# DeltaNet core: identity folded into the fp16 matrices, half-width inversion levels, and two heads side by side

## What is computed

```python
L = where(strict, einsum('bhncd,bhnsd->bhncs', k * beta, k) * decay, 0)
sol = triangular_solve(eye + L, concatenate([v * beta, k * beta * exp(g)]))
u, w = split(sol)
qk = where(tril, einsum('bhncd,bhnsd->bhncs', q, k) * decay, 0)
def step(S, xs):
    v_new = u_i - einsum('bhcd,bhde->bhce', w_i, S)
    o = einsum(qd_i, S) + einsum(qk_i, v_new)
    S = S * gl_i + einsum('bhcd,bhce->bhde', kd_i, v_new)
```

## Time and profile before

| | |
|---|---|
| median of 3 runs | 5612.43 us (5612.35 to 5614.2) |
| span of the profiled execution | 5611.9 us |
| PE, PEld, DVE, ACT, POOL busy | 4687.5, 3852.9, 3332.0, 2146.1, 2161.1 us |
| the phase of the delta core | about 1840 to 3932 us of the span |
| mean granted TensorE clock | 0.925 of full speed |

### The profile page before, as it was taken

One profiled execution on the slowest core, in us unless ns is written; L12 is line 12 of the kernel. 1 busy time (PEld: TensorE's weight loads), 2 busy tenths in 40 slices (PEclk: granted clock), 3 DMA queues, 4 the chain that ended last, 5 costly groups with the idle time before them and its releaser, 6 DMA issues. The chain is left out here.

```text
span 5611.9 us, 92238 instructions
## 1 busy us (share of the span) xinstructions
PE 4687.5 (84%) x32058; PEld 3852.9 (69%) x32058; DVE 3332.0 (59%) x3990; ACT 2146.1 (38%) x3371; POOL 2161.1 (39%) x1544
## 2 busy tenths in 40 slices
PE   7479889988998688888888888888599759975649
PEld 1467777777777577777777777777488548864547
DVE  1414543455334688888888888888455443339854
ACT  0212222232223455555555555555211231137732
POOL 0311111111121666777666767675211132213222
PEclk8569999999999899999999999999799879987879
DMA  4102212212222333333333333332544212221134
GB/s 203 48 25 70 58 49 69 81 46 64 65 69 62 92 95 95 92 92 92 95 95 94 92 93 93 95 93 77 186 174 177 102 54 68 66 94 69 67 103 135
DMA packets 587420, 503.28 MB, mean 90 GB/s; under 512 B 115200, under 2 KB 556544, under 8 KB 573184
## 3 DMA queue, kind: packets, MB, share of 16 engines
q1 hardware_dynamic: 587296, 501.82, 29.7%
HBM read 351.00 MB, written 150.67 MB: 89 GB/s over the span
## 5 line engine op out<-in xcount | busy, mean ns | idle before, releaser
L448 PE MATMUL pj_bank<-h_hi,pj_whi 128*128 128x512 f32 (+1 forms) x1920 | 716.5, 373 | 19.7 <-POOL pj_wlo L434 19.7
L448 PE MATMUL pj_bank<-h_lo,pj_whi 128*128 128x512 f32 (+1 forms) x1920 | 707.8, 369 | 0.0
L448 PE MATMUL pj_bank<-h_hi,pj_wlo 128*128 128x512 f32 (+1 forms) x1920 | 707.3, 368 | 0.0
L1215 DVE TENSOR_TENSOR dc_Y<-dc_psY,dc_levels 128x512 f16<-128x512 f32 x864 | 554.3, 683 | 117.3 <-PE dc_psY L996 113.8
L1219 DVE TENSOR_TENSOR dc_X<-dc_psX,dc_X 128x512 f16<-128x512 f32 x864 | 575.8, 690 | 79.6 <-PE dc_psX L1010 48.4
L431 POOL TENSOR_TENSOR pj_whi<-pj_w,ones 128x1024 fp32r<-128x1024 f32 x48 | 126.8, 2642 | 1192.4 <-DMA pj_w<-in_gdn_w_in 959.0
L1129 ACT ACTIVATE dc_R<-dc_psR 128x512 f16<-128x512 f32 x864 | 492.5, 596 | 123.2 <-PE dc_psR L1006 112.8
L622 ACT ACTIVATE pj_raw<-pj_bank 128x512 f32<-128x512 f32 (+1 forms) x240 | 129.0, 555 | 1005.6 <-PE pj_bank L448 634.9
L448 PEld LDWEIGHTS pj_bank<-h_hi,pj_whi 128*128 128x128 f32 x1920 | 362.9, 189 | 82.9 <-POOL pj_wlo L434 20.1
L912 POOL TENSOR_TENSOR dc_bm<-dc_dec,dc_bm 128x512 f32<-128x512 f32 x144 | 183.3, 1273 | 588.1 <-ACT dc_dec L1106 587.9
L448 PEld LDWEIGHTS pj_bank<-h_lo,pj_whi 128*128 128x128 f32 x1920 | 363.0, 189 | 62.6 <-issue 3.8
(11 more groups left out here) (239 smaller groups left out, 11155.3 us busy)
## 6 DMA issues: line engine op xcount, KB each, us to landing
dc_tm<-scratch_tm SPq DMA_DIRECT2D x288, 192.0 KB, 2.4
dc_fm<-scratch_fm SPq DMA_DIRECT2D x288, 128.0 KB, 2.6
dc_cgr<-scratch_cgrow SPq DMA_DIRECT2D x288, 128.0 KB, 2.9
scratch_o<-dc_ob SPq DMA_DIRECT2D x288, 128.0 KB, 1.9
scratch_tm<-pj_tm SPq DMA_DIRECT2D x24, 1152.0 KB, 6.3
mod_w<-in_mod_w SPq DMA_DIRECT2D x16, 1536.0 KB, 30.2
pj_w<-in_gdn_w_in SPq DMA_DIRECT2D x48, 512.0 KB, 7.4
scratch_fm<-pj_row SPq DMA_DIRECT2D x16, 1152.0 KB, 6.0
```

The costliest lines, as they stand in the source:

```text
L448: i = pe.matmul(self.bank[blk][:, 0:n], l[b][:, k, :], r[:, k, at:at + n], start=(m == 0), stop=(m == 3 * KT - 1))
L1215: dve.tensor_tensor(Y[p][:], bY[p][:], lev_r(l + 1), ALU.mult).then_inc(eY[p], 1)
```

## The change

Only `phase_delta_core` changes. Its parts are:

1. **Half columns.** A level of block size s = 2^l changes only half of the columns of R and X, the other half only of Y. Y, R and X products of levels 2 to 6 are now made for 64 of the 128 columns of each of the four problems, side by side in 256 columns of a bank (`quart`), and the copies out of PSUM take those 256 elements and write them to their places in the 512 (`all_cols`, runs of s elements). Products of Y and the first transposes (`first`) are half wide from the start; R and X of level 1 are full.
2. **Identity inside.** A = Lhi + I in fp16, Y keeps the identity in the columns that are not written (one Y tile for each level, filled once at the start), so that X Y alone is the new R and the identity products of the levels (L1004) and of the error (L1018) go. X is no longer an addition on DVE but a copy: level 1 on DVE, levels 2 to 6 on ACT.
3. **Level 0** is made by masking A instead of multiplying and adding: still two fp16 operations on DVE, both with two SBUF inputs.
4. **Making.** `gram` is read once from PSUM by DVE under a mask of both triangles (`masked`, new, 128x512); ACT's copy L1115 and POOL's L907 and L913 go. `scores` now has two SBUF inputs.
5. **Two heads side by side.** p = 0 and 1 are two different q/k heads at the same chunk, so that each has its own state, and only the banks Z and V tie them. The order of the pieces of the recurrence in a level changes accordingly.
6. **SyncE** issues the same 28 transfers in an iteration, written out for all 72 without a loop, at other distances ahead (recurrence 1, `fm` 3, rows 4).

```diff
+        quart = lambda t: t[:].rearrange("p d h t -> p (d h t)")[:, 0:2 * P]
+        def cols(t, c, l, own):
+            o = (c // 2 == 0) == own
+            return comb(t, c).rearrange("p (b o s) -> p b o s", o=2, s=1 << l)[:, :, 1 if o else 0, :]
+        def all_cols(t, l, of_r):
+            s = 1 << l
+            at, step = (s, 2 * P - s) if of_r else (0, 2 * P + s)
+            a = t[:]
+            return bass.AP(tensor=a.tensor, offset=a.offset + at, ap=[[4 * P, P], [step, 2], [2 * s, P // s], [1, s]])
+        def split4(v, l):
+            return v.rearrange("p (d b s) -> p d b s", d=2, s=1 << l)
+        pick, x0m = sb("pick", [P, LV] + H4[1:], F16), sb("x0m", [P, 2, P], F16)
+        R0 = two("R0", H4, F16)
+        Y = [two(f"Y{l}_", C4, F16) for l in range(1, NLEV)]
...
                 def level_y(j, q, l, p):
+                    for c in range(4):
+                        m = pe.matmul(quart(bY[p])[:, c * 64:(c + 1) * 64], comb(A[q][p], c),
+                                      half(R0[p], c) if l == 1 else cols(R[p], c, l, True), start=True, stop=True)
...
                 def level_rx(j, l, p):
-                    pe.matmul(flat(bR[p]), id16[:, 0:P], flat((R0 if l == 0 else R)[p]), start=True, stop=False)
+                    for c in range(4):
+                        if l == 1:
+                            m = pe.matmul(comb(bR[p], c), comb(X0[p], c), comb(y, c), start=True, stop=True)
+                        else:
+                            m = pe.matmul(quart(bR[p])[:, c * 64:(c + 1) * 64], comb(X[p], c), cols(y, c, l, True), start=True, stop=True)
...
                 def newton_e(j, q, p):
-                    pe.matmul(flat(bY[p]), id16[:, 0:P], flat(R[p]), start=True, stop=False)
...
                 @sweep
                 def run(i, q, ahead, make, inv, rec):
+                    for l in range(1, NLEV):
+                        if inv:
+                            for p in range(2):
+                                level_y(j, r, l, p)
+                        if rec and l <= 2:
+                            state_by_k(i, q, l - 1)
+                        if rec and l in (3, 4):
+                            solved(i, l - 3)
+                        if rec and l == 6:
+                            update(i, q, 1)
+                        if inv:
+                            for p in range(2):
+                                level_rx(j, l, p)
+                        if make and l <= 2:
+                            gram(i + 2, q, l - 1)
+                        if rec and l == 4:
+                            update(i, q, 0)
+                        if rec and l >= 5:
+                            outputs(i, q, 0, l - 5)
...
                 def level_x(j, l, p):
+                    act.activation(all_cols(X[p], l, False), split4(quart(bX[p]), l), ACT.Copy).then_inc(eX[p], 1)
...
                 def masked(j, q, p):
+                    dve.tensor_tensor(gm[q][p][:], bV[:], sides[:], ALU.mult).then_inc(s_gm[p], 1)
                 def level(j, l, p):
-                    dve.tensor_tensor(Y[p][:], bY[p][:], lev_r(l + 1), ALU.mult).then_inc(eY[p], 1)
+                    dve.tensor_tensor(all_cols(Y[l - 1][p], l, True), split4(quart(bY[p]), l),
+                                      split4(pick[:, l - 1].rearrange("p c t -> p (c t)"), l), ALU.mult).then_inc(eY[p], 1)
```

More of the change, by code:

```diff
@@ L766, in phase_delta_core @@
[L766 to L773, removed]
@@ L805, in run @@
                     for q in range(2):
                         body(m * 2 + q, q, True, True, True, True)
-                for i in range(NPAIR - 4, NPAIR):
+                for i in range(NI - 4, NI):
                     at(i)
             return run
[L811 to L817, removed]
@@ new lines, in store, with step @@
+                def store(m, n, p):
+                    row = m * 2 + p
+                    wait(sp, s_ob[p], m * NCH + n + 1)
+                    for dr in range(2):
+                        dst = dram["o"][dr, chunk(dr, n)].rearrange("p (q h) t -> p q h t", h=2)[:, bass.ds(row, 1)]
+                        sp.dma_start(dst.rearrange("p o h t -> p (o h) t"), ob[p][:, dr]).then_inc(s_out[p], 16)
+                def step(m, n, last):
+                    for load, ahead in ((load_rec, 1), (load_fm, 3), (load_row, 4)):
+                        if not (last and n + ahead >= NCH):
+                            for p in range(2):
+                                load(*place(m, n, ahead), p)
+                    for p in range(2):
+                        store(m, n, p)
@@ L967, in _ @@
+                    for p in range(2):
+                        if ahead:
+                            differences(i + 3, 1 - q, p)
+                        if make:
+                            low(i + 2, q, p)
+                        if inv:
+                            beta_v(i + 1, 1 - q, p)
                 run(pool)
@@ new lines, in run @@
+                            if l == 1:
+                                for p in range(2):
+                                    level_x(j, p)
+                        if rec and l == 1:
+                            right_side(i, q, 0)
+                        if rec and l in (3, 4):
+                            faded_v(i, q, l - 3)
+                        if make and l in (1, 2):
+                            masked(i + 2, q, l - 1)
+                        if rec and l == 2:
+                            right_side(i, q, 1)
@@ L1267, in run @@
+                        if make and l in (3, 4):
+                            scores(i + 2, q, l - 3)
+                        if make and l in (5, 6):
+                            first(i + 2, q, l - 5)
+                        if rec and l == 5:
+                            state(i, q, 0)
+                    if rec:
+                        state(i, q, 1)
                     if inv:
```

614 lines of the change are left out of this document (299 added, 315 removed).

## The result

The changed kernel takes 5250.9 us (median of 4 runs, 5248.2 to 5253.1) against 5613.3 us before (4 runs): ratio 0.935, 95% interval 0.934 to 0.937. I had forecast 5395 us, with a range of 5280 to 5520. The sign was right; the size was wrong, and so was the range. The change saved 362 us where I had 217.

What follows compares the result with a forecast made beforehand. It took a PE, DVE, PE, ACT chain on two nearly full engines as the bound; iterations of 28.56 us becoming 25.5 save 3.06 us times 71, 217 us, so 5611.9 becomes 5395 us, range 5280 to 5520.

Steps and rivals of the forecast that it cites:

- the term for PE: PE work per delta-core iteration: 24.1 to 21.0 us, identity groups gone, narrow products left at 0.056 us each.
- the walked 25.5: Delta-core iteration length in us, from following the chain of waits: 24.4 plus about 1.1 for blocked A and X0.
- The stall: A and X0 of step 0 on DVE, blocked by POOL through shared SBUF ports: about 1.1 us more per iteration.
- The identity products: On PE, dropping the identity groups of 12 RX saves 2.64 us per iteration, those of two errors 0.44.
- The DVE term: DVE work per iteration falls from 24.1 to 15.9 us, with a 256-element copy from PSUM at 0.46 us.
- The DMA: The 28 transfers per iteration need about 15 us of 25.5 to issue and stay hidden.
- +3 and -3: Outside the iterations: 3 us more for set-up operations on DVE, 3 us less for the shorter lead-in.
- Cheaper than walked: Rival, chance 0.12: narrow products under 0.056 us, or A ahead of POOL; iterations 24.0 us or less, under 5290 us.
- The clock: Rival, chance 0.06: PE's granted clock drops to 1.2 GHz in the core; about 31.5 us per iteration, 5820 us.
- Weight loads: Rival, chance 0.04: narrow PE products follow by the 0.098 us of a load; 30 us per iteration, 5715 us.
- Scattered writes: Rival, chance 0.04: 34 narrow copies slowed by scattered writes, some 3 us; 28.5 us per iteration, 5610 us.
- Dearer chain: Rival, chance 0.12: costlier hand-overs or Y copies at 0.68 us; 27 to 28.3 us per iteration, 5500 to 5590 us.

Runs made afterwards that it cites:

- f1: The changed kernel with the products of levels 2 to 6 back on all 128 columns, copies still narrow: 5346.4 us.
- h1: The changed kernel with POOL's differences and Llo waiting for both X0, and beta times v moved up to finish before A starts: 5194.3 us.
- e2: The changed kernel with the 512-column identity product put back ahead of R X in all six levels, its output overwritten: 5380.2 us.
- e3: The changed kernel with every narrow copy of levels 1 to 6 made twice, first into a tensor nobody reads: 5609.0 us.
- f2: The changed kernel with each narrow product of levels 1 to 6 issued as two 32-column products, same weights loaded twice: 5369.9 us.
- k1: The changed kernel with 128-column products in levels 2 to 6 and the identity product ahead of R X both restored: 5495.5 us.
- g2: The changed kernel with Llo on POOL after beta times v and both X0, and right side 1 before the second masked gram on DVE: 5240.2 us.

## Why the prediction was wrong

**The step that failed** is the term for PE: "Halving columns saves nothing further in my sum: a product of 64 columns still loads 128 weights, and I leave it at the 0.056 us at which loads follow now. The floor would be half that." The floor was the value. 136 narrow products at 0.029 make 3.7 us less, so PE's work is some 17.3 us and not 21.0. f1 gives 120 of the 136 their columns back and costs 1.35 us per steady iteration; scaled to 136, an estimate, that is 1.5 of the 1.94 us between the walked 25.5 and the measured 23.56, or some 109 of the 144 us by which I was off. I read the pace of the loads from rows in which products of 128 columns ran, so it was the products' pace all along; nothing in the earlier trace rows bounded the load from below, and I had kept both ends but then took the dear one, on a mechanism that no row showed.

**The stall**: mechanism right, size off. I charged 1.1 us per iteration (0.7 more on both A and X0 of step 0); of the two only X0 is caught, and h1 puts the price at 0.84 steady. (In step 1 both are, A at 1.00 and X0 at 1.26, but no group above waits for state 1.) The pair of step 0:

```profile
2725.80 0.42 DVE L1233 TENSOR_TENSOR dc_A<-dc_Lhi,dc_id 128x512 f16<-128x512 f16 x1
2726.26 1.26 DVE L1236 TENSOR_TENSOR dc_X<-dc_A,dc_x0m 128x512 f16<-128x512 f16 x1
```

That is 0.26 us per iteration, 18 us more of the miss. "The second operation is caught whoever wins the first" held here.

**The rest** of the miss I can't assign: some 0.15 us per steady iteration, 11 us, and about 6 us outside the steady iterations. No run tested it.

**What held.** The length of an iteration is what the waits make of it: no engine is over 84%, and the named waits are all there (L1053, L1063, L1041, L1221). The identity products: 2.64 us of work, of which e2 finds 1.79 in the chain. The DVE term: 413 ns instead of 460. The DMA stayed hidden: between 1940 and 3500 us of the kernel after no engine waited for one. The first `scores` start 5.4 us later than before (1859.3 against 1853.9), and what follows the last is 4.7 us shorter (1725.2 against 1729.9), so +3 and -3 can't be told apart: the first `scores` of the other kernels start anywhere from 1852.1 to 1859.6.

**Rivals.** *Cheaper than walked* came true, by the first of its two mechanisms, "narrow products at less than 0.056 us"; I gave it 0.12. I wrote that PE's last third, from 15.6 us on, would give most of it; in fact 1.1 of the 1.94 us are gained by then. *The clock*: 1.00 in the window, out. (The products of 64 columns in the gates phase are no close likeness: they are fp32 and last 0.40 us each in the trace before, 0.19 here.) It fell in e3 (0.95, PE 77% busy) and a little in f2 (0.98, PE 88% busy, most products the shortest), while k1 (91%) and g2 (82%) kept 1.00, so it was not far off; what decides it these runs don't settle. *Weight loads*: out, four loads in 0.18 us. *Scattered writes*: out, 382 and 413 ns. *Dearer chain*: out.

**The range** ended at 24.0 us per iteration. With the floor of the product term in it, which f1 prices at 1.35 to 1.5 us in the chain, it would have ended near 22.6, 5189 us, and held the result.

## What to carry to other kernels

When a price is taken from a stream of pairs, ask which half of the pair sets the pace; if the rows can't say, both values belong in the range. A stall through shared ports was cured here only when the neighbour engine had no operation at all in that place: look for the next one in its queue. Doubling an operation into a scratch tensor measures how much of it lies in the chain, without knowing the chain. Compare iterations of the same granted clock: an edit can move the clock too, and a mean over the run then mixes the two.
